# Feed-forward of a four-stage network: residual by an identity product, norm out of the banks, first two hidden tiles token-major

## What is computed

```
ALPHA_2 = (2.0 * DEPTH) ** 0.25          # DEPTH = 2
D_FF = ((8 * D_MODEL // 3 + 127) // 128) * 128   # 2816
...
def swiglu(x, w_gate, w_up, w_down):
    return (jax.nn.silu(x @ w_gate) * (x @ w_up)) @ w_down
...
    for l in range(DEPTH):
        x = layer_norm(ALPHA_2 * x + 0.5 * swiglu(x, ffn1_gate[l], ffn1_up[l], ffn1_down[l]), ln_g[l, 0], ln_b[l, 0])
...
        x = layer_norm(ALPHA_2 * x + mix, ln_g[l, 1], ln_b[l, 1])
        x = layer_norm(ALPHA_2 * x + 0.5 * swiglu(x, ffn2_gate[l], ffn2_up[l], ffn2_down[l]), ln_g[l, 2], ln_b[l, 2])
```

## Time and profile before

| | us |
|---|---|
| median of 3 runs (lowest, highest) | 2324.59 (2318.47, 2326.11) |
| profiled execution, first to last instruction | 2323.1 |
| PE busy | 2166.1 (93%) |
| DVE busy | 1142.2 (49%) |
| ACT busy | 784.0 (34%) |
| mean granted TensorE clock | 0.975 |

### The profile page before, as it was taken

How to read it: one execution, slowest core, us unless ns; L and a number is a source line. 1 busy time by engine, 2 the same in 40 slices (tenths; PEclk the granted TensorE clock), 3 DMA queues, 4 the chain that set the end, 5 groups by cost and what they waited for, 6 DMA issues and landing times.

```text
span 2323.1 us, 30109 instructions
## 1 busy us (share of the span) xinstructions
PE 2166.1 (93%) x12126; PEld 1528.0 (66%) x12126; DVE 1142.2 (49%) x1786; ACT 784.0 (34%) x1299; POOL 61.5 (3%) x62
## 2 busy tenths in 40 slices
PE   8999998899887989997988999999999999989998
PEld 7884443443367944433433688898888788888887
DVE  5582222121156831211111666678666766787666
ACT  3441110111034321101111355454555455554553
POOL 0010000000010100000000000001000000001000
PEclk9999999899998799999999999999999999999999
DMA  9449999999972289999999864634555464534561
GB/s 289 145 175 379 421 421 421 417 421 420 413 246 73 76 363 420 420 421 415 420 420 421 295 209 168 199 128 127 181 200 200 154 208 166 193 96 159 167 208 46
DMA packets 231542, 622.66 MB, mean 268 GB/s; under 512 B 15456, under 2 KB 166944, under 8 KB 182112
## 3 DMA queue, kind: packets, MB, share of 16 engines
q1 hardware_dynamic: 226096, 605.32, 68.7%
q0 software_dynamic: 3040, 10.78, 1.5%
q10 hardware_dynamic: 2256, 4.50, 0.5%
HBM read 619.51 MB, written 1.05 MB: 267 GB/s over the span
## 4 chain that ended last, share of the span: by engine, by line
PE 41%; DMA 6%; DVE 4%; ACT 2%; issue 1%; POOL 0%; SPq 0%; DVEq 0%; ACTq 0%
PE bank L1517 14%; PE bank L1505 10%; PE bank L1518 7%; PE bank L228 6%; PE bank L1345 3%; DMA arena<-in_moe_w_up 1%; DMA ring<-in_moe_w_up 1%; DMA ring<-in_ffn_gate 1%; DMA w_parts<-in_moe_w_up 1%; DMA x_tok<-in_moe_w_up 1%; DVE w_low L439 1%; PE bank L1673 1%; ACT w_high L432 1%; DVE x_tok L687 0%; DVE x_tok L676 0%
## 5 line engine op out<-in xcount | busy, mean ns | idle before, releaser
L439 DVE TENSOR_TENSOR w_low<-ring,w_high 128x1024 fp32r<-128x1024 f32 x364 | 441.1, 1225 | 271.7 <-ACT w_high L432 271.7
L1517 PE MATMUL bank<-xT_parts,w_high 128*128 128x512 f32 x1408 | 496.2, 395 | 6.0 <-DVE xT_parts L504 6.0
L432 ACT ACTIVATE w_high<-ring 128x1024 fp32r<-128x1024 f32 x364 | 377.1, 1053 | 218.0 <-PE bank L1518 184.6
L1518 PE MATMUL bank<-xT_parts,w_low 128*128 128x256 f32 x1408 | 394.5, 280 | 0.0
L1345 PE MATMUL bank<-ring,arena 128*64 128x512 f32 x1344 | 339.0, 594 | 17.3 <-DMA w_parts<-in_moe_w_gate 5.3
L1517 PEld LDWEIGHTS bank<-xT_parts,w_high 128*128 128x128 f32 x1408 | 264.0, 188 | 69.0 <-DVE xT_parts L504 6.9
L1345 PE MATMUL bank<-w_parts,arena 128*64 128x512 f32 x768 | 263.8, 609 | 13.4 <-DMA w_parts<-in_moe_w_up 6.7
L1518 PEld LDWEIGHTS bank<-xT_parts,w_low 128*128 128x128 f32 x1408 | 265.8, 189 | 3.1
L1345 PEld LDWEIGHTS bank<-ring,arena 128*64 128x64 f32 x1344 | 110.1, 137 | 230.5 <-issue 221.9
L1453 DVE SCALAR_TENSOR_TENSOR arena<-arena,bank 128x512 f32<-128x512 f32 x32 | 23.9, 747 | 434.1 <-PE bank L1345 434.1
L228 PE MATMUL bank<-w_high,xT_parts 128*128 128x256 f32 x1152 | 222.9, 290 | 10.4 <-DVE w_low L439 8.8
(11 more groups left out here) (284 smaller groups left out, 2934.4 us busy)
## 6 DMA issues: line engine op xcount, KB each, us to landing
ring<-in_moe_w_gate SPq DMA_DIRECT2D x56, 1024.0 KB, 24.3
ring<-in_moe_w_up SPq DMA_DIRECT2D x56, 1024.0 KB, 21.0
ring<-in_moe_w_down SPq DMA_DIRECT2D x56, 1024.0 KB, 25.8
ring<-in_ffn_gate SPq DMA_DIRECT2D x44, 1024.0 KB, 6.8
ring<-in_ffn_up SPq DMA_DIRECT2D x44, 1024.0 KB, 5.4
ring<-in_ffn_down SPq DMA_DIRECT2D x44, 1024.0 KB, 6.6
w_parts<-in_moe_w_up SPq DMA_DIRECT2D x32, 1024.0 KB, 26.1
w_parts<-in_moe_w_down SPq DMA_DIRECT2D x32, 1024.0 KB, 26.1
```

The lines of the kernel that those rows point to most:

```text
L432: e.activation(hi, src, ACT.Copy).then_inc(*S.high.tell(key))
L439: e.tensor_tensor(lo, src, hi.bitcast(F32), ALU.subtract).then_inc(*S.low.tell(key))
L1517: e.matmul(pairs(bank[:, :]), hi[:, j, :], k.x_parts[:, :, j, :], start=j == 0, stop=False)
L1518: ins = e.matmul(bank[:, 0:T], lo[:, j, :], k.xh[:, j, :], start=False, stop=j == KT - 1)
```

## The change

- **Residual.** DVE's scaling of x and its four adds go. `residual_pe` opens banks 0 to 3 at the start of the stage with an identity product of `x_tok`, two per block, in fp32, and the down products accumulate on it. The hidden values are multiplied by 0.5 / ALPHA (in an instruction that is there already), so the bank holds the sum divided by ALPHA; the norm's epsilon is divided by ALPHA squared.
- **Norm.** bn_stats and the centre read the banks; the centre is two halves.
- **Tiles 0 and 1.** Their gate and up are computed token-major, each block by itself: x's parts stand in the array, 256 weight columns stream by, 24 products for a block and name. A weight part is now half of the rows with the columns of both tiles. The hidden block is transposed on PE (`first_hidden_pe`), and the order ahead of the stage is gate 0, gate 1, up 0, up 1. The two up parts get buffers of their own, `second0` in the arena and `second1` over `mixT`.
- **Order.** `ffn_pe` takes over the transposes: block 0, residual, gate of block 0, block 1's transposes, up of block 0, residual, gate of block 1, up of block 1. The norms ahead of a feed-forward make block 0's low parts before they centre block 1, then split the up parts, then make block 1's low parts. `norm_after_experts_dve` is shared with the second mixer of the first block, which thereby gets the same order.
- **Fillers.** `BUSY_AHEAD` has none ahead of a feed-forward but after the experts: 4 before block 0, 1 before its gate, 2 before block 1.

```diff
+HALF_SHARE = 0.5 / ALPHA
...
+BUSY_AHEAD = {"mixer": (0, 0, 0), "experts": (4, 1, 2), "ffn": (0, 0, 0)}
...
+def first_block_pe(e, k, i, name, n, tb, busy=0):
...
+    bank = k.banks.open(e, B_BANKS, ("ffn", i, name + " sum", tb))
+    if tb == 0:
+        e.wait_ge(*S.low[keys[1]])
+    if name == "gate":
+        busy_pe(e, k, bank, busy)
+        x_ready(e, k, n, tb)
...
+def residual_pe(e, k, i, tb):
+
+    for half in range(2):
+        bank = k.banks.open(e, (2 * tb + half,), ("ffn", i, "out", tb, half))
+        e.matmul(bank[:, :], k.ident, k.x_tok[:, tb, BANK * half:BANK * half + BANK], start=True, stop=False)
...
-                        ins = e.matmul(out, lhs, rhs[:, 0, cols], start=g == 0 and j == 0, stop=g == FT - 1 and j == 2)
+                        ins = e.matmul(out, lhs, rhs[:, 0, cols], start=False, stop=g == FT - 1 and j == 2)
...
-    for f in range(FT):
+    busy = BUSY_AHEAD[after]
+    transpose_block_pe(e, k, n, 0, busy[0])
+    residual_pe(e, k, i, 0)
+    first_block_pe(e, k, i, "gate", n, 0, busy[1])
+    transpose_block_pe(e, k, n, 1, busy[2])
+    first_block_pe(e, k, i, "up", n, 0)
+    residual_pe(e, k, i, 1)
+    first_block_pe(e, k, i, "gate", n, 1)
+    first_hidden_pe(e, k, i, 0)
+    first_block_pe(e, k, i, "up", n, 1)
+    for f in range(2, FT):
...
+    for tb in range(NB):
+        e.wait_ge(*first_done(S, i, "gate", tb))
+        e.activation(k.ffn_gate[:, tb, :], k.banks["ffn", i, "gate sum", tb][:, 0:T], ACT.Silu).then_inc(*S.act_out.tell(("ffn", i, "gate sum", tb)))
+    ffn_fill(e, k, i, 4, 8, split_act)
...
-        e.tensor_scalar(k.acc[:, tb, :], k.x_tok[:, tb, :], ALPHA, None, ALU.mult).then_inc(*S.dve_step.tell(("scaled", i, tb)))
...
-    e.scalar_tensor_tensor(out=k.acc[:, tb, cols], in0=k.banks["ffn", i, "out", tb, half][:, :], scalar=0.5, in1=k.acc[:, tb, cols],
-                           op0=ALU.mult, op1=ALU.add).then_inc(*S.dve_out.tell(("ffn", i, "out", tb, half)))
...
+    e.bn_stats(k.bn[:, tb, 6 * half:6 * half + 6], k.banks["ffn", i, "out", tb, half][:, :]).then_inc(*S.norm_step.tell((norm, tb, "half", half)))
...
-def norm_after_experts_dve(e, k, X, n):
+def norm_after_experts_dve(e, k, X, n, ahead):
...
+    norm_mean_dve(e, k, n, 1)
+    for key in ahead[0]:
+        split_dve(e, k, key)
+    first_block_dve(e, k, n)
+    for key in ahead[1]:
+        split_dve(e, k, key)
+    x_low_dve(e, k, n, 1, 0)
+    x_low_dve(e, k, n, 1, 1)
```

More of the change, by code:

```diff
@@ L316, in split_parts @@
         for f in range(FT + FFN_LAG):
-            own += [("ffn", i, "gate", f), ("ffn", i, "up", f)] if f < FT else []
+            if f == 0:
+                own += [("ffn", i, name, part) for name in ("gate", "up") for part in range(2)]
+            own += [("ffn", i, "gate", f), ("ffn", i, "up", f)] if 2 <= f < FT else []
             own += [("ffn", i, "down", f - FFN_LAG)] if f >= FFN_LAG else []
@@ L464, with transpose_block_pe @@
 BUSY = {"mixer": (0, 4), "experts": (4, 4), "ffn": (0, 4)}
+BUSY_AHEAD = {"mixer": (0, 0, 0), "experts": (4, 1, 2), "ffn": (0, 0, 0)}
+def transpose_block_pe(e, k, n, tb, busy=0):
+    S = k.S
+    if n < 0:
+        e.wait_ge(*S.x_loaded[tb][0])
+    for half in range(2):
+        view = pairs(k.banks.open(e, B_BANKS, ("xT", n, tb, half))[:, :], 4)
+        if half == 0:
+            busy_pe(e, k, k.banks["xT", n, tb, half], busy)
+        if n >= 0:
+            e.wait_ge(*S.x_tok[n, tb, half])
+        for i in range(4):
+            ins = e.transpose(view[:, i, :], k.x_tok[:, tb, block(4 * half + i)], k.ident)
+        ins.then_inc(*S.turned.tell((n, tb, half)))
 def transpose_x_pe(e, k, n, after=None):
-    S = k.S
     for tb in range(NB):
[L470 to L480, removed]
+        transpose_block_pe(e, k, n, tb, BUSY[after][tb] if n >= 0 else 0)
 def x_parts_at(k, n, tb, half):
@@ L1519, in ffn_pe @@
             ins.then_inc(*S.used.tell(key))
+            if f == 2 and name == "gate":
+                first_hidden_pe(e, k, i, 1)
         if f >= FFN_LAG:
             g = f - FFN_LAG
-            if g == 0:
-                for tb in range(NB):
-                    for half in range(2):
-                        k.banks.open(e, (2 * tb + half,), ("ffn", i, "out", tb, half))
             down((0, 1), (0, 1), [g]).then_inc(*S.used.tell(("ffn", i, "down", g)))
@@ L1536, in ffn_act @@
 def ffn_act(e, k, i):
-    S, n = k.S, 4
-    for f in range(FT):
+    S, n = k.S, 8
+    key = "ffn", i, "turned", 0
+    for tb in range(NB):
+        e.wait_ge(*first_done(S, i, "gate", tb))
+        e.activation(k.ffn_gate[:, tb, :], k.banks["ffn", i, "gate sum", tb][:, 0:T], ACT.Silu).then_inc(*S.act_out.tell(("ffn", i, "gate sum", tb)))
+    ffn_fill(e, k, i, 4, 8, split_act)
+    e.wait_ge(*S.product["ffn", i, "turned", 1])
+    e.activation(k.hid_high[:, 0:2, :], pairs(k.banks[key][:, :]), ACT.Copy).then_inc(*S.ffn_high.tell((i, 1)))
+    for f in range(2, FT):
         for name, out in (("gate", k.ffn_gate), ("up", k.ffn_hidden)):
```

186 lines of the change are left out of this document (119 added, 67 removed).

## The result

The changed kernel takes 2328.62 us, the median of 20 runs (2323.39 to 2331.83); the kernel before took 2324.86 over as many. The ratio is 1.0022 with a 95% interval of 1.0016 to 1.0029: 3.7 to 6.7 us slower, 5.1 in the middle; the two medians lie 3.8 apart, the two means 5.0. So 20 runs tell 0.2% from no change, where the prediction thought of 0.3%. The forecast was +5.2 and 2329.8, within 0.3% of before, and so it came out.

The account below looks back on a forecast made before the run. PE, never idle inside a feed-forward, was taken as the bound, so only its work and the hand-overs count. Terms 0.1 + 1.1 + 6.8 + 1.5 - 0.9 - 0.7 - 2.7 = +5.2 gave 2329.8 us, range 2320 to 2336.

Parts of the forecast that it names:

- Start of FFN 0: After the experts: PE waits 4.4 for the up parts, tile 2 comes 6.8 us later, low clock adds 1.5.
- rival without that wait: At FFN 0 the up parts get done in time; sum -0.7, 2324 us; chance 0.11.
- The other starts: Tile 2 comes 0.1 us later at FFN 2 and 0.55 later at each of FFN 1 and FFN 3.
- Block 1's residual: At each feed-forward start, block 1's residual products on PE cost 1.72 us.
- slower rival: Clock also falls at the other feed-forward starts, 1.5 us each; three make +9.7, 2334 us; chance 0.24.
- Norms out of a feed-forward: Into the mixer, twice: 0.73 us earlier without the add, centre 0.25 longer, so -0.45 each.
- The end, -0.7: At the program's end the residual add goes and all behind it is one chain: 0.7 us less.
- od, -2.7: Experts to second mixer: start 1.4 us earlier, clock holds for 1.5 more, 0.15 taken back: 2.7 less.
- faster rival: No FFN 0 wait and no low clock at 1500 to 1504 (-1.5): sum -2.2; beyond -7, chance 0.05.

Follow-up runs that it names:

- combined kernel: Changed kernel with FFN 0's up parts split early, no fillers between blocks there, block 1's residual before block 0's up product: 2315.35 us, ratio 0.9965; again 0.9968.

## Why the prediction was right, and where it was not

**Start of FFN 0, +6.8 and +1.5 for the clock.** Right in place, mechanism and size: the wait was 4.17 for 4.4, tile 2 came 7.84 later for 8.3. Three runs split it: 1.58 is clock, 5.93 goes with the wait and the clock together, 1.74 is the fillers. The rival without that wait falls.

**The other starts, +0.1 and +0.55 twice.** By the same reckoning (tile 2, with 11.18 for the two tiles of before) they are -0.28, +0.28 and +0.29. The forecast counts in the second pair of hidden transposes, which stand behind tile 2's first products and take 0.13 or 0.14; with them it is -0.15, +0.42 and +0.43, so the steps were 0.1 to 0.3 too high. The wait before the up product was there, 0.1 to 0.2 shorter than forecast. The mis-sized terms are small: the up product of FFN 2 starts 7.74 behind the transposes for 7.89, and a pair of hidden transposes takes 0.13 for 0.22. Block 1's residual, 1.72 in the sum, was right: taking it out moved tile 2 by 1.70 where the clock stayed at 1.00. The segments of FFN 1 and FFN 2 come out lower still, +0.05 and -0.50, because tiles 3 and 4 now run at the faster of the two paces of the last section. That the clock would fall at these starts too, the slower rival, did not happen: 1.00 at all three.

**Norms out of a feed-forward, -0.45 each.** The first product of the mixer stands 7.01 behind the transposes instead of 7.44 and 7.45: -0.43 and -0.44.

**The end, -0.7.** From the last product to the end it was 8.60 (2314.50 to 2323.1) and is 7.54 (2317.96 to 2325.5): -1.06. The step left out a wait. Before, scale 1 waited 0.51 for the reciprocal root on POOL, which runs beside the centre; now the chain above has 0.03 ahead of the scale. The two profiles, centre, root and, before, the scale:

```profile
2316.71 1.27 DVE L676 SCALAR_TENSOR_TENSOR x_tok<-acc,mv,norm_gb 128x1024 f32<-128x1024 f32 x1
2316.87 1.52 POOL L695 TENSOR_TENSOR rstd<-var_eps,tables 128x1 f32<-128x1 f32 x1 [4.07 <-DVE var_eps L674]
2318.49 1.42 DVE L687 SCALAR_TENSOR_TENSOR x_tok<-x_tok,rstd,norm_gb 128x512 f32<-128x512 f32 x2 [0.51 <-POOL rstd L695]
...
2319.45 1.41 DVE L1688 SCALAR_TENSOR_TENSOR x_tok<-bank,mv,norm_gb 128x512 f32<-128x512 f32 x2
2319.61 0.55 POOL L717 TENSOR_TENSOR rstd<-var_eps,tables 128x1 f32<-128x1 f32 x1 [5.03 <-DVE var_eps L690]
```

The longer centre alone would not have covered it: with the old 1.52 the root would be ready at 2321.13, behind the scale's start at 2320.90. The root itself takes 0.55 beside a centre that reads the banks (last section). Of the 1.06 the add gives 0.72; the rest is the wait that is gone, less the longer centre.

**od, -2.7.** This step failed in size. The start came 1.4 earlier and the clock held, both as said, but the segment gained 1.7 over all profiles. Part of the 2.7 is still there at a wait that all 13 profiles have early in the mixer: it ends at 35.30 to 35.32 behind the transposes with the old order and at 32.68 to 33.47 with the new one, 1.8 to 2.6 sooner. The profiles with the least gain have a new wait of up to 0.50 for a weight part at 25.5 to 25.8, where old ones have none. The rest is lost between 78 and 94 (old) or 76 and 92 (new): that stretch takes 15.2 to 16.4 with the old order and 15.7 to 16.4 with the new one, and the mean granted clock in it is 0.81 in before and 0.82 in the changed kernel, so part of it is at the low level either way. I had counted a gain at the start as a gain at the end.

**What was not in the sum.** Both profiles of before lose clock once between the start of FFN 0 and 4 us into the mixer behind it; in the eleven profiles with the norm out of the banks that mixer takes 118.08 to 118.39, so none loses it there. I had this only as part of the faster rival (-1.5). By the profiles at hand it makes up for od; how often before loses it over all its runs, two profiles don't tell. The forecast of the sum, +5.2, thus stands on one large term that was right, several small ones that were 0.1 to 0.4 too high each, one that was 1.0 too good and one of about the same size that was missing. That these cancel is luck.

**Where the gain went.** The part that takes work off DVE pays: alone 0.9983, of which about 1 us is the pace. The part that was to start PE sooner, tiles 0 and 1 by blocks, costs 8.1 at FFN 0 (6.1 against the second profile of before), because its order on ACT was not changed with it. With order, fillers and residual mended it is 0.9965.

## What to carry to other kernels

When work is moved forward on one engine, walk each engine that feeds it: an in-order engine with 8 us of idle time can still deliver last, because the piece that is needed stands behind one that waits. Extra products on the bounding engine are free as far as they stand in a wait, so place them by the waits in the trace. Fillers belong in the wait itself; ahead of work that others wait for they only delay it.

## What the runs showed of the hardware that was not expected

The low clock moves. The same kernel had its low stretch at 1500 in one profile and at 1304 in another, and the combined kernel had one or two in the second layer's mixer (126.47 and 128.98). A low stretch seen in one profile is no fixed cost of that place, unless a long wait of PE stands right ahead of it. Behind the waits of 4.03 to 4.17 it came in every profile where the wait was left empty, and in neither where it was filled; behind the 2.59 at od it came in all four profiles with the old order. Behind 2.09 in the run without residual it came at FFN 1 and not at FFN 3.

The same pair of products (512 and 256 columns) runs at one of two paces at granted clock 1.00, from one start to the next: 0.3536 in tiles 0 to 4 of FFN 1 and 2 of before (in FFN 1 the first down product starts 35.51 behind the transposes), 0.3467 in those of FFN 0 and 3 and of FFN 1 in the kernel with residual and norm alone (35.00, the first tile at 7.18 in both). That is 0.5 us per stage and explains the shorter segment there. From about tile 5 on every stage changes between the two from tile to tile. In the changed kernel tile 2 begins at the slow pace and goes on at the fast one behind the two hidden transposes that stand in it, and tiles 3 and 4 keep it. What sets the pace was not tried.

POOL's reciprocal root also has two durations, and which one comes goes with the DVE operation beside it. In all 13 profiles it takes 1.46 to 1.53 in the 143 cases where that operation has no bank among its operands (the old centre, the split of a weight part), and ends 0.40 to 0.43 behind it; it takes 0.54 to 0.56 in the 117 cases where the operation reads a bank (the centre of the change, the low part of x). So a norm out of the banks shortens the chain on POOL too. The first kind of operation has 1024 columns and the second 512, and no run changes the one without the other.
